# Memory attention's prompt scores from three rounded products of split operands

## The reference, cut to what matters

```
def memory_block(x, mk, mv, norm_mem_q, w_mem_q, w_mem_o):
    q = (rmsnorm(x, norm_mem_q) @ w_mem_q).reshape(bsz, L, MEM_HEADS, MEM_HEAD_DIM)
    s = jnp.einsum('bqhd,bkhd->bhqk', q, mk).astype(jnp.float32) * (MEM_HEAD_DIM ** -0.5)
    p = jax.nn.softmax(s, axis=-1).astype(mv.dtype)
    o = jnp.einsum('bhqk,bkhd->bqhd', p, mv).reshape(bsz, L, D_MODEL)
    return x + o @ w_mem_o
```

## Time and profile before

| | |
|---|---|
| median of three runs | 1180.42 us |
| the profiled execution | 1179.15 us, its span 1177.4 us |
| PE busy (products) | 1122.1 us, 95% |
| PEld busy (weight loads) | 1014.3 us, 86% |
| DVE busy | 805.8 us, 68% |
| ACT busy | 608.2 us, 52% |
| POOL busy | 124.5 us, 11% |
| chain that ended last | PE 75%, DVE 9%, ACT 8%, issue 4%, DMA 3% |
| PE records of the plain scores (line 3290) | 80 of 128 or 64 rows by 256 columns, 687.9 to 787.0 us |

### The profile page before, as it was taken

The page is one execution under the profiler, slowest core; times in us unless marked ns, Lnnn a source line. Parts: engine busy times, 40 slices in busy tenths (PEclk is TensorE's granted clock), DMA queues, the critical chain, the costliest instruction groups (busy, mean ns, idle before and its releaser), DMA issues.

```text
span 1177.4 us, 18680 instructions
## 1 busy us (share of the span) xinstructions
PE 1122.1 (95%) x7757; PEld 1014.3 (86%) x7766; DVE 805.8 (68%) x993; ACT 608.2 (52%) x807; POOL 124.5 (11%) x148
## 2 busy tenths in 40 slices
PE   6999999999999899899999999999899999999995
PEld 6988789999987799899999999989767878788884
DVE  6324665865968887987535733534589998899895
ACT  6334463335397576643215523312166768677773
POOL 2002431000245000000000000000001000000032
PEclk9999999999999999999999999999799999999998
DMA  9431110323120344442627602201799999999988
GB/s 300 136 120 37 37 41 1 109 72 121 30 55 1 87 123 117 133 151 76 220 72 239 225 3 72 73 1 55 292 353 382 421 419 386 375 400 390 375 274 200
DMA packets 94655, 205.26 MB, mean 174 GB/s; under 512 B 4336, under 2 KB 70040, under 8 KB 81640
## 3 DMA queue, kind: packets, MB, share of 16 engines
q1 hardware_dynamic: 85792, 173.88, 41.6%
q0 software_dynamic: 5584, 19.81, 5.7%
q10 hardware_dynamic: 3192, 10.34, 2.2%
HBM read 182.41 MB, written 21.61 MB: 173 GB/s over the span
## 4 chain that ended last, share of the span: by engine, by line
PE 75%; DVE 9%; ACT 8%; issue 4%; DMA 3%; ACTq 0%; POOL 0%; SPq 0%; DVEq 0%; POOLq 0%
PE ps L2765 34%; PE ps L3101 10%; PE ps L1112 6%; DVE buf_r L1046 4%; ACT buf_r L1039 3%; PE ps L1122 3%; PE ps L3290 2%; PE ps L3306 2%; DMA buf<-in_w_gate_e 1%; PE ps L2886 1%; ACT buf_r L507 1%; DVE buf_r L1261 1%; PE ps L2915 1%; PE ps L2928 1%; PE ps L2916 1%
## 5 line engine op out<-in xcount | busy, mean ns | idle before, releaser
L2765 PE MATMUL ps<-buf_r,buf_r 128*128 128x288 f32 (+1 forms) x3312 | 435.7, 291 | 6.2 <-ACT buf L1812 2.6
L2765 PEld LDWEIGHTS ps<-buf_r,buf_r 128*128 128x128 f32 x3312 | 423.4, 189 | 10.3 <-issue 6.7
L1046 DVE TENSOR_TENSOR buf_r<-buf,buf_r 128x2048 fp32r<-128x2048 f32 x92 | 205.1, 2284 | 0.0
L1112 PE MATMUL ps<-buf_r,buf_r 128*128 128x512 f32 x720 | 174.6, 397 | 0.0
L1039 ACT CAST buf_r<-buf 128x2048 fp32r<-128x2048 f32 x92 | 170.8, 1909 | 0.0
L1112 PEld LDWEIGHTS ps<-buf_r,buf_r 128*128 128x128 f32 x720 | 133.2, 188 | 29.7 <-issue 0.5
L3101 PE MATMUL ps<-buf_r,buf_r 128*128 128x288 f32 x1008 | 140.2, 299 | 9.3 <-ACT buf L1977 4.4
L3101 PEld LDWEIGHTS ps<-buf_r,buf_r 128*128 128x128 f32 x1008 | 137.3, 192 | 11.1 <-issue 9.2
L492 DVE TENSOR_TENSOR buf_r<-buf,buf_r 128x2048 fp32r<-128x2048 f32 (+1 forms) x33 | 74.5, 2262 | 36.2 <-ACT buf_r L486 36.1
L486 ACT CAST buf_r<-buf 128x2048 fp32r<-128x2048 f32 (+1 forms) x37 | 69.7, 1883 | 56.7 <-PE ps L2789 39.7
L1122 PE MATMUL ps<-buf_r,buf_r 128*128 128x512 f32 x384 | 89.8, 389 | 0.5 <-DVE buf_r L1289 0.5
(11 more groups left out here) (367 smaller groups left out, 1521.6 us busy)
## 6 DMA issues: line engine op xcount, KB each, us to landing
buf<-in_w_gate_e SPq DMA_DIRECT2D x32, 1024.0 KB, 8.2
buf<-in_w_up_e SPq DMA_DIRECT2D x32, 1024.0 KB, 7.5
buf<-in_w_down_e SPq DMA_DIRECT2D x32, 1024.0 KB, 7.6
buf<-in_w_in SPq DMA_DIRECT2D x16, 1024.0 KB, 5.5
buf<-in_w_in SPq DMA_DIRECT2D x17, 512.0 KB
buf<-in_w_mem_kv SPq DMA_DIRECT2D x8, 1024.0 KB, 6.2
y_rows<-buf ACTq DMA_DIRECT2D x14, 512.0 KB, 7.1
buf<-in_x_prompt SPq DMA_DIRECT2D x8, 512.0 KB, 5.3
```

Source lines behind the costliest of these rows:

```text
L1046: nc.vector.tensor_tensor(e_lo(t), e_raw(t), e_hi(t), ALU.subtract).then_inc(wl_ready, 1)
L1112: last = nc.tensor.matmul(bank(b), r32(a[:, k, :]), w[:, i, :], start=(k == 0 and j == 0), stop=(k == KD - 1 and j == 2))
L2765: last = nc.tensor.matmul(out, a, b, start=(k == 0 and j == 0), stop=(k == len(parts) - 1 and j == 2))
```

## The change

The four prompt blocks' scores, steps 0 to 15, are formed with `passes`: three rounded products for each of the two plain ones, six passes in all. For these, ACT's new `query_high(a)` rounds the step's 128x256 queries into `QS[a % 2]` and counts `qs_high`; DVE's new `query_low(a)` waits for that, subtracts, writes `QS_LOW[a % 2]` and counts `qs_low`, for which `mscores(a)` now waits. Both are issued two steps ahead: ACT has `query_high(a + 2)` in step a behind the exponential and the fill's `query_out`, DVE has `query_low(a + 2)` in step a behind the scaling. `query_high(0)` stands behind `query_out(1)`, and `query_high(1)` behind `query_out(3)`; `query_low(0)` stands between the two weight splits ahead of the steps, `query_low(1)` behind them. The prompt's keys are copied to fp32r and DVE subtracts a low part `KM_LOW` from PSUM. `KM_LOW` lies over the new tokens' raw keys, `MC[:, 0]`, and so these keys are turned first. The steps of the new tokens (16 to 19) stay in plain fp32. The renamed counters `row_stats` joins `nm_ready` and `rr_ready`; `Q_ROWS` is another name of `Q_MEM`.

```diff
+        QS = [A.view(2, P) for _ in range(2)]
+        QS_LOW = [A.view(2, P) for _ in range(2)]
...
+        KM_LOW = MC[:, 0].rearrange("p m (c n) -> p (m c) n", n=ML)
...
+            def query_high(a):
+                m, h = divmod(a, 4)
+                act.wait_ge(q_ready, Q_ROWS + (0 if m < 2 else KD) + 2 * (h + 1))
+                if a >= 2:
+                    act.wait_ge(ms_psum, a - 1)
+                nc.scalar.copy(r32(QS[a % 2]), QM[:, 2 * h:2 * h + 2, m * P:(m + 1) * P]).then_inc(qs_high, 1)
+
             query_out(0)
             split_high(act, W_MQ + 2)
             query_out(1)
+            query_high(0)
             split_high(act, W_MQ + 3)
             for j in range(2, Q_FIRST):
                 query_out(j)
+            query_high(1)
             for a in range(STEPS):
...
                     for j in Q_FILL[a]:
                         query_out(j)
+                if a + 2 < 4 * (NC_ - 1):
+                    query_high(a + 2)
...
-            for b in range(4):
-                s, m = divmod(b, 2)
-                dve.wait_ge(km_psum, b + 1)
-                nc.vector.tensor_copy(KM[:, s, :, m * P:(m + 1) * P],
-                                      bank(2 * (b % 2), 2).rearrange("p (c n) -> p c n", c=KD)).then_inc(km_ready, 1)
+            keys = lambda m: bank(2 * m, 2).rearrange("p (c n) -> p c n", c=KD)
+            for m in range(2):
+                dve.wait_ge(km_psum, m + 1)
+                nc.vector.tensor_copy(KM[:, 1, :, m * P:(m + 1) * P], keys(m)).then_inc(km_ready, 1)
+            for m in range(2):
+                dve.wait_ge(km_psum, m + 3)
+                nc.vector.tensor_copy(r32(KM[:, 0, :, m * P:(m + 1) * P]), keys(m)).then_inc(km_ready, 1)
+                dve.wait_ge(km_ready, 2 * m + 3)
+                nc.vector.tensor_tensor(r32(KM_LOW[:, :, m * P:(m + 1) * P]), keys(m), r32(KM[:, 0, :, m * P:(m + 1) * P]),
+                                        ALU.subtract).then_inc(km_ready, 1)
+
+            def query_low(a):
+                m, h = divmod(a, 4)
+                dve.wait_ge(qs_high, a + 1)
+                nc.vector.tensor_tensor(r32(QS_LOW[a % 2]), QM[:, 2 * h:2 * h + 2, m * P:(m + 1) * P], r32(QS[a % 2]),
+                                        ALU.subtract).then_inc(qs_low, 1)
+
             split_low(dve, W_MQ + 2)
+            query_low(0)
             split_low(dve, W_MQ + 3)
+            query_low(1)
...
                 nc.vector.tensor_scalar(PX[a % 2][:n, :], PX[a % 2][:n, :], RR[:n, a:a + 1], None, ALU.mult).then_inc(pn_ready, 1)
+                if a + 2 < 4 * (NC_ - 1):
+                    query_low(a + 2)
...
-                src = MKV[:, m, 0:D] if s == 0 else MC[:, 0, m, :]
+                src = MC[:, 0, m, :] if s == 0 else MKV[:, m, 0:D]
...
-            pe.wait_ge(km_ready, 4)
+            pe.wait_ge(km_ready, 6)
...
-                pe.wait_ge(q_ready, Q_MEM + (0 if m < 2 else KD) + 2 * (h + 1))
+                if m < NC_ - 1:
+                    pe.wait_ge(qs_low, a + 1)
+                else:
+                    pe.wait_ge(q_ready, Q_ROWS + KD + 2 * (h + 1))
                 if a >= 2:
                     pe.wait_ge(px_ready, a - 1)
-                for j in range(2):
-                    last = nc.tensor.matmul(bank(a % 2)[:n, 0:ML], QM[:, 2 * h + j, t0:t0 + n],
-                                            KM[:, 0 if m < 4 else 1, 2 * h + j, :], start=(j == 0), stop=(j == 1))
+                if m < NC_ - 1:
+                    qs, qs_rest = r32(QS[a % 2]), r32(QS_LOW[a % 2])
+                    km, km_rest = r32(KM[:, 0, 2 * h:2 * h + 2, :]), r32(KM_LOW[:, 2 * h:2 * h + 2, :])
+                    last = passes(bank(a % 2)[:, 0:ML], [((qs[:, j, :], qs_rest[:, j, :]), (km[:, j, :], km_rest[:, j, :]))
+                                                         for j in range(2)])
+                else:
+                    for j in range(2):
+                        last = nc.tensor.matmul(bank(a % 2)[:n, 0:ML], QM[:, 2 * h + j, t0:t0 + n], KM[:, 1, 2 * h + j, :],
+                                                start=(j == 0), stop=(j == 1))
```

More of the change, by code:

```diff
@@ L199, in encoder_step @@
         HI_MO = [A.view(WT)]
+        QS = [A.view(2, P) for _ in range(2)]
+        QS_LOW = [A.view(2, P) for _ in range(2)]
+        assert A.at <= spot - KD * ML
         A.back(spot - KD * ML)
@@ L535, in encoder_step @@
         mkv_psum, mkv_rows, km_psum, km_ready = (sem(n) for n in ("mkv_psum", "mkv_rows", "km_psum", "km_ready"))
[L536 to L539, removed]
+        Q_MEM = Q_ROWS = 4
+        (ms_psum, row_stats, px_ready, qs_high, pn_ready, pt_psum, pt_ready, ot_psum, qs_low) = (
+            sem(n) for n in ("ms_psum", "row_stats", "px_ready", "qs_high", "pn_ready", "pt_psum", "pt_ready",
+                             "ot_psum", "qs_low"))
         mo_psum, x2_ready = sem("mo_psum"), sem("x2_ready")
@@ L2111, in _ @@
                 query_out(j)
+            query_high(1)
             for a in range(STEPS):
                 n = CH[a // 4][1]
-                act.wait_ge(nm_ready, a + 1)
+                act.wait_ge(row_stats, 2 * a + 1)
                 if a >= 2:
@@ L2692, in _ @@
                 dve.wait_ge(ms_psum, a + 1)
-                nc.vector.tensor_reduce(NEGM[:n, a:a + 1], bank(a % 2)[:n, 0:ML], AX.X, ALU.max, negate=True).then_inc(nm_ready, 1)
+                nc.vector.tensor_reduce(NEGM[:n, a:a + 1], bank(a % 2)[:n, 0:ML], AX.X, ALU.max, negate=True).then_inc(row_stats, 1)
                 if a >= 1:
@@ L2698, in _ @@
                 dve.wait_ge(px_ready, a + 1)
-                nc.vector.reciprocal(RR[:n, a:a + 1], RS[:n, a:a + 1]).then_inc(rr_ready, 1)
-                dve.wait_ge(rr_ready, a + 1)
+                nc.vector.reciprocal(RR[:n, a:a + 1], RS[:n, a:a + 1]).then_inc(row_stats, 1)
+                dve.wait_ge(row_stats, 2 * a + 2)
                 nc.vector.tensor_scalar(PX[a % 2][:n, :], PX[a % 2][:n, :], RR[:n, a:a + 1], None, ALU.mult).then_inc(pn_ready, 1)
+                if a + 2 < 4 * (NC_ - 1):
+                    query_low(a + 2)
                 if a % 2 and a >= 3:
@@ L3266, in query_half @@
                 if j >= 2:
-                    pe.wait_ge(q_ready, Q_MEM + j - 1)
+                    pe.wait_ge(q_ready, Q_ROWS + j - 1)
                 n, c = W_MQ + i // 2, (i % 2) * P
@@ L3317, in mem_rows @@
                 if i == 0:
-                    pe.wait_ge(q_ready, Q_MEM + 16)
+                    pe.wait_ge(q_ready, Q_ROWS + 16)
                 if i >= 2:
```

## The result

The changed kernel takes 1185.08 us (median of 22 runs, 1181.98 to 1191.28) against 1180.45 for the kernel before in the same session (22 runs, 1178.11 to 1189.21). The ratio, taken over all runs and not from the two medians (whose quotient is 1.0039), is 1.0035, 95% interval 1.0022 to 1.0047: slower by 0.35%, where 0.28% was forecast, with a chance of 0.71 on a change within 0.5%.

A forecast was written before the change was run, and what follows sets the result against it. PE was taken to bound the kernel, with no gap in the attention steps; - 2.4 (passes) + 4.8 (queries) + 0.95 (keys) = + 3.35 us gave 1183.8 us, 8-in-10 range 1177.2 to 1188.8.

The forecast's parts named there:

- part 2: Queries' split on ACT and DVE: its order makes PE wait at scores 2 to 11, 4.8 us in all.
- the seven: Scores 4 to 10, queries taken out earlier: PE waits 0.40 us each, bounds 0.37 to 0.64.
- the sum: PE's total over the score passes, queries' split and keys: + 3.35 us, bounds + 2.0 to + 6.8.
- part 1: Prompt score passes on PE: six rounded replace four plain, saving 0.15 us a step, 2.4 us in 16 steps.
- part 3: Keys' subtractions on DVE ahead of the steps: scores 1 wait 0.95 us, bounds 0.75 to 1.2.
- What is queued behind: DVE's work behind the waiting subtraction, up to the turns' scaling: costs nothing, 1.5 us of cover left.
- rival B: At PE's turns: next step's maximum behind the waiting subtraction makes the softmax late; 1188.8 us, chance 0.12.
- The carry to the end: Expert stage after the memory stage: weight transfers follow PE, so the shift reaches the end whole.
- rival C: In the expert stage: the shift is absorbed because experts wait for weights; 1180.4 us, chance 0.07.
- Rival A: At the scores: copy and subtraction are hidden, so the saving lands whole; 1178.0 us, chance 0.12.
- rival D: In the stretch with waits: PE's clock falls through the new waits; 1189.3 us, chance 0.05.

The follow-up runs named there:

- e1_order: Changed kernel with ACT's rounding copy of the queries ahead of the fill's take-out in steps 2 to 8; stage 93.90 us, ratio 1.0019 to before.
- e2_low_twice: Changed kernel with DVE's subtraction of the queries' low part issued twice in a row; stage 102.13 us, ratio 1.0089 to before.
- e3_plain: Changed kernel with all copies, subtractions and waits, but prompt scores formed by plain fp32 products; stage 99.01 us, ratio 1.0041 to before.
- e4_keys_alone: Kernel before plus only the keys' part: new tokens' keys turned first, two DVE subtractions, scores plain; stage 93.31 us, no ratio taken.
- e5_first6: Changed kernel with six query halves ahead of the steps instead of four, copies ahead of take-outs; stage 92.87 us, ratio 1.0000 to before.
- b_again: Kernel before, unchanged, profiled a second time to see how much profiles vary; stage 93.30 us against 93.26 in its first profile.

## Why the prediction was right

**The chain at the scores (part 2).** Right in each term. Read from the ends of the query fills in the two chains of waits, the step of scores 4 to 10 became 0.26 to 0.27 us longer (forecast 0.40 - 0.15 = 0.25), that of scores 3 and 11 0.40 (0.55 - 0.15), and that of scores 2 0.78 (0.9 - 0.15). Scores 12 to 15, costed at nothing, made their steps 0.14 us shorter each. The assumption that only ACT's order bound scores 4 to 10 was shown by e1_order, which took 2.88 us away by that order alone. That DVE's subtraction is the last link was shown by e2_low_twice. One bound was miscounted: by its own terms the most for one of the seven is 0.62 us, not 0.64, which takes 0.14 off the upper end of the sum and changes nothing else.

**The passes (part 1).** Right: 0.72 to 0.73 for six, 0.87 for four plain ones; 0.14 a step in e3_plain against 0.15 forecast. This is where the sum was a little low: the step lengths give 5.76 us of added waiting, as forecast (5.75), less 2.24 instead of 2.4 saved, which is the stage's 3.52. The Trainium skill, FP8 and Floating Point Precision, section TensorE Precision Notes, counts true FP32 as four passes; by that alone a step would have given 0.22, an estimate (a quarter of 0.87). The number of passes is only part of it: a plain product took 0.43 us, a quarter of it is 0.108, and a rounded pass in these streams took 0.12.

**The keys (part 3).** The 0.95 us at scores 1 was right: the stretch with scores 0 and 1 is 0.65 us longer, which is 0.95 less two steps' saving of 0.15. Its cause is a near tie. The timeline of the changed kernel:

```profile
689.90 2.28 DVE L496 TENSOR_TENSOR buf_r<-buf,buf_r 128x2048 fp32r<-128x2048 f32 x1
691.38 0.41 ACT L2108 ACTIVATE buf<-ps 128x288 f32<-128x288 f32 x1 [2.81 <-PE ps L2796]
691.82 0.40 ACT L2115 CAST buf_r<-buf 128x256 fp32r<-128x256 f32 x1
692.26 0.42 DVE L2694 TENSOR_TENSOR buf_r<-buf,buf_r 128x256 fp32r<-128x256 f32 x1
```

DVE's split ends at 692.18 and ACT's copy at 692.22. The heading of part 3 was misleading in one point: the wait belongs to the queries' chain, and the keys only make DVE late enough to tie. By these rows the copy would have held the subtraction without them; that the keys cost nothing by themselves was shown on the kernel before (e4_keys_alone), not on the changed one. How thin the tie is shows in e2_low_twice, where 0.4 us more on DVE ahead of the split made scores 1 later by 0.3.

**What is queued behind.** Costed at nothing, and nothing it was: no wait at the turns (rival B). The cover was larger than the prediction's 1.5 us. Step 5 of the changed kernel:

```profile
729.28 0.35 DVE L2730 TENSOR_SCALAR buf<-buf,buf 128x256 f32<-128x256 f32 x1
...
731.41 0.25 PEld L3382 LDWEIGHTS ps<-buf,buf 128*128 128x128 f32 x2
```

The scaling ended 1.78 us ahead of the turns' load, against 1.81 in the earlier trace rows; in steps 5 to 9 it was 1.77 to 1.82 against 1.81 to 1.88, and in e2_low_twice, with the subtraction doubled, 1.98 to 2.24. In PE's order the next scores, which wait for the subtraction, stand ahead of the turns, so the turns are put off along with DVE's queue and the cover isn't used up. The wait of 1.2 us in e5_first6 is no measure of this cover: the step there has no query half to fill it, and the weight rounding and the half split stand in its chain, not the subtraction.

**The carry to the end.** Assumed whole. The stage grew by 3.5 us and the total by the ratio 1.0035, 4.1 us with an interval from 2.6 to 5.5; e2_low_twice, with 8.9 and 10.5 us (8.4 to 12.6), agrees, and the time behind the stage was no shorter there. So rival C, that the delay is absorbed whole, fell. The 4.6 us between the medians is more than the stage's 3.5; whether any of the rest is real isn't settled by these runs, since the interval holds 3.5.

**The others.** Rival A fell with the eleven waits, rival D with the granted clock, which was 1.00 in every ten microseconds of the changed kernel from 690 to 780.

## What to carry to other kernels

An operation of 0.4 us on an engine that is half idle costs what the place in that engine's queue makes it cost: ask which instruction ahead of it waits for the bottleneck engine, add up the chain back to that engine, and subtract the other work the bottleneck has meanwhile. If its inputs are ready earlier, put it ahead of the instruction that waits. After such a repair look for the next hole, since moving the filling work away from one step opened a wait of 1.2 us in another. And for sums of a few us measure one stage between two marks of the trace, which repeated to 0.07 us here while spans of the same kernel differed by 6.

## What the runs showed of the hardware

The granted clock of PE differed between executions with the same instructions. The windows of 160 to 180 us, first of the kernel before in its first profile, then in b_again:

```profile
160.00:180.00 20.00, 20.00 (x158) 18.20 (x158) 14.62 (x14) 11.65 (x10) 8.06 (x9) 1.00 0.00 1
```
```profile
160.00:180.00 20.00, 20.00 (x119) 18.05 (x119) 9.95 (x10) 8.63 (x8) 5.45 (x4) 0.74 0.00 1
```

PE was busy throughout both, at a mean granted clock of 1.00 and 0.74 (the levels are 2.4 and 1.2 GHz), and got through 158 and 119 of its products. In 120 to 160 us it was the other way round, 0.91 and 1.00. The turn just ahead of the stage came at anywhere from 675.7 to 680.3 us over thirteen profiles, all with the same instructions up to the keys. How much of that the clock makes isn't shown: these two profiles reached the turn within 0.15 us of each other.
